# Pair phase of an RWKV-7/GLA block kernel: written-out pair loop, deferred head norm, projection work moved into the scan, turns as identity products

## The reference, cut to what matters

```python
def _rwkv_scan(r, decay, k, v, a_vec, b_vec, s0, reverse, emit):
    """RWKV-7 state recurrence S <- S diag(w) + (S a) b^T + v k^T, y = S r."""
...
decay = jnp.exp(-jnp.exp(-jax.nn.softplus(-w_log) - 0.5))
iclr = jax.nn.sigmoid(lp["a_a0"] + jnp.einsum("btdr,drc->btdc", la, lp["a_a2"]))
kk = kk * lax.rsqrt(jnp.sum(kk * kk, axis=-1, keepdims=True) + 1e-12)
...
mu = jnp.mean(wkv, axis=-1, keepdims=True)
var = jnp.mean(jnp.square(wkv - mu), axis=-1, keepdims=True)
y_a = ((wkv - mu) * lax.rsqrt(var + A_LN_EPS)).reshape(bsz, t, A_WIDTH) * lp["a_lnx_g"] + lp["a_lnx_b"]
bonus = jnp.einsum("bthn,btdhn,hn->bth", f["r"], f["k"], lp["a_r_k"])[..., None] * f["v"]
y_a = (y_a + bonus.reshape(bsz, t, A_WIDTH)) * jax.nn.silu(f["z_a"])
```

## Time and profile before

| What | us |
|---|---|
| median of three runs | 2912.06 |
| the profiled execution, own time | 2906.06 |
| its span, first to last instruction | 2904.3 |
| TensorE busy in the span | 2618.7 (90%) |
| GpSimd, ScalarE, VectorE busy | 1421.1, 1114.5, 1013.6 |
| first product of pair 0 (L551) | 314.9 |
| last VectorE operation of pair 7 (L1059) | 1104.1 |
| mean granted clock of TensorE | 0.956 of full speed |

### The profile page before, as it was taken

The page is one execution under the profiler, slowest core; times in us unless marked ns, Lnnn a source line. Parts: engine busy times, 40 slices in busy tenths (PEclk is TensorE's granted clock), DMA queues, the critical chain, the costliest instruction groups (busy, mean ns, idle before and its releaser), DMA issues.

```text
span 2904.3 us, 68141 instructions
## 1 busy us (share of the span) xinstructions
PE 2618.7 (90%) x27478; PEld 2337.1 (80%) x27478; DVE 1013.6 (35%) x1692; ACT 1114.5 (38%) x1642; POOL 1421.1 (49%) x623
## 2 busy tenths in 40 slices
PE   7997879887987978999999997998999989999998
PEld 5665766665775667877899996998998989999997
DVE  0215845555564542333211113333332133233311
ACT  0103333333333323344444434544444454454443
POOL 0006212122121103444688885776666867776785
PEclk9999989899998978999999998999999999999999
DMA  8682111111111102222555552444444534444453
GB/s 302 225 280 89 62 40 40 54 41 45 41 48 45 38 17 68 87 87 87 194 180 182 186 182 73 154 163 152 150 140 137 186 111 159 166 152 159 159 176 121
DMA packets 97980, 361.43 MB, mean 124 GB/s; under 512 B 10880, under 2 KB 12032, under 8 KB 97440
## 3 DMA queue, kind: packets, MB, share of 16 engines
q1 hardware_dynamic: 97488, 355.85, 36.7%
q10 hardware_dynamic: 336, 3.15, 0.3%
HBM read 356.85 MB, written 2.10 MB: 124 GB/s over the span
## 4 chain that ended last, share of the span: by engine, by line
PE 70%; issue 7%; ACT 6%; DVE 5%; POOL 4%; ACTq 0%; DVEq 0%; POOLq 0%
PE ps L193 16%; PE ps L195 15%; PE ps L194 15%; PE ps L488 4%; POOL wlo L181 3%; PE ps L490 3%; PE ps L489 3%; ACT whi L171 2%; PE ps L580 1%; PE ps L567 1%; PE ps L551 1%; PE ps L1483 1%; PE ps L622 1%; DVE W L881 1%; POOL alo L1517 1%
## 5 line engine op out<-in xcount | busy, mean ns | idle before, releaser
L181 POOL TENSOR_TENSOR wlo<-raw,whi 128x1024 fp32r<-128x1024 f32 x566 | 1371.7, 2442 | 1407.0 <-ACT whi L171 1397.2
L193 PE MATMUL ps<-ahi,whi 128*128 128x256 f32 (+1 forms) x3760 | 1118.8, 298 | 66.9 <-POOL wlo L181 29.9
L194 PE MATMUL ps<-alo,whi 128*128 128x256 f32 (+1 forms) x3760 | 1099.5, 292 | 0.0
L195 PE MATMUL ps<-ahi,wlo 128*128 128x256 f32 (+1 forms) x3760 | 1099.1, 292 | 0.0
L193 PEld LDWEIGHTS ps<-ahi,whi 128*128 128x128 f32 x3760 | 728.9, 194 | 102.2 <-POOL wlo L181 38.0
L171 ACT ACTIVATE whi<-raw 128x1024 fp32r<-128x1024 f32 x566 | 585.4, 1054 | 431.0 <-PE ps L195 260.1
L195 PEld LDWEIGHTS ps<-ahi,wlo 128*128 128x128 f32 x3760 | 729.8, 194 | 10.0
L194 PEld LDWEIGHTS ps<-alo,whi 128*128 128x128 f32 x3760 | 730.1, 194 | 9.6
L488 PE MATMUL ps<-ahi,whi 128*128 128x256 f32 (+1 forms) x512 | 206.7, 404 | 0.7 <-ACT W L787 0.7
L312 PE MATMUL ps<-raw,small 128*2 128x128 f32 x1536 | 174.0, 276 | 21.9 <-DMA raw<-stream 14.3
L312 PEld LDWEIGHTS ps<-raw,small 128*2 128x2 f32 x1536 | 131.0, 86 | 65.1 <-DMA raw<-stream 14.8
(11 more groups left out here) (303 smaller groups left out, 2947.2 us busy)
## 6 DMA issues: line engine op xcount, KB each, us to landing
raw<-stream SPq DMA_DIRECT2D x662, 512.0 KB, 3.3
W<-xT SPq DMA_DIRECT2D x1, 4096.0 KB, 17.9
XR<-xT ACTq DMA_DIRECT2D x1, 2048.0 KB, 7.6
outT<-XR SPq DMA_DIRECT2D x4, 512.0 KB, 2.7
W<-pair_par SPq DMA_DIRECT2D x8, 146.0 KB, 2.9
cns<-consts SPq DMA_DIRECT2D x1, 1120.0 KB, 5.3
cns<-consts ACTq DMA_DIRECT2D x1, 896.0 KB, 10.1
W<-gk_w ACTq DMA_DIRECT2D x1, 128.0 KB, 2.4
```

What stands on the lines that cost most here:

```text
L181: nc.gpsimd.tensor_tensor(wlo[slot], raw[slot], whi[slot].bitcast(F32), ALU.subtract).then_inc(lo_done, 1)
L193: nc.tensor.matmul(out, whi[slot][:, k, :], mh, start=first and k == 0, stop=False)
L194: nc.tensor.matmul(out, whi[slot][:, k, :], ml, start=False, stop=False)
L195: ins = nc.tensor.matmul(out, wlo[slot][:, k, :], mh, start=False, stop=last and k == UK - 1)
```

## The change

The loops over pairs become Python loops, so that every pair is straight code on every engine except GpSimd's. AL and RHO, the parameters and the decays get two buffers each, by the pair's parity; the other AL buffer serves as X, and TW (the decay's logarithm) shares the buffer of the next pair's AL. The ScalarE copy of the parameters goes away, SP loads them straight into the buffer in front of the pair's fifth unit. The parts:

- **Norm.** The tail's operations of pair i-1 stand in the inverse of pair i: sum and deviation between the maskings, mean behind the third square, variance in level 1, logarithm behind the first turned copies, exponential before the copy of BE, the gated result in level 3. Five VectorE operations become three.
- **Inverse.** A level multiplies MB by X first and turns X behind it; the turn is sixteen 64x64 products with an identity per direction into banks 6 and 7 (one half bank for both directions, so the second turn waits for the copy of the first). BE, KA and V are turned by the same kind of products (32, 32 and 16). No projection piece stands in the inverse, and of VectorE's next-pair work none but six of the twelve operations of the value convolution.
- **Scan.** All 48 pieces, in the portions of FILL. The low-rank products come in two halves (w before the scan, a in step 1). Decays, both other convolutions, key norm, AL, RHO and DECS stand between the state updates. The next taken-in products (L640) move behind the state update. The bonus product stands before the scan.

```diff
+        FILL = ((3, 2, 3), (3, 2, 3), (3, 2, 3), (3, 2, 3), (1, 1, 2), (1, 1, 2), (1, 1, 2), (1, 3, 0))
-            def turn(d):
-                for b in range(4):
-                    ins = nc.tensor.transpose(ps[:, 2 + 2 * d, P * b:P * b + P], X[:, d, P * b:P * b + P], ident)
-                ins.then_inc(R["t_mm"].sem, 1)
+            def turn(d):
+                for h, a, e, b in cells():
+                    o = (h * 2 + a) * C
+                    ins = nc.tensor.matmul(ps[side(e), 6 + b, o:o + C], X[side(b), d, cell(h, a, e)],
+                                           ident[side(b), side(b)], start=True, stop=True)
+                ins.then_inc(R["t_mm"].sem, 1)
+            def to_tokens(vec):
+                for d in range(2):
+                    for c in range(8):
+                        for h in range(2):
+                            o = (d * 4 + c // 2) * C
+                            ins = nc.tensor.matmul(ps[side(c % 2), h, o:o + C], vec[side(h), d, chunk(c)],
+                                                   ident[side(h), side(h)], start=True, stop=True)
             square(KA, AL, 6).then_inc(R["prod_k"].sem, 1)
-            fill(10)
+            if i:
+                nc.tensor.matmul(ps[:, 0, 0:T], headw, ysum, start=True, stop=True).then_inc(R["mean_mm"].sem, 1)
             R["ev_mb"].wait(pe, i * 2 + 2)
-            for d in range(2):
-                R["ev_x"].wait(pe, i * 2 + d + 1)
-                turn(d)
             for lv in range(1, LEVELS + 1):
                 for d in range(2):
-                    R["xt_ev"].wait(pe, i * 10 + (lv - 1) * 2 + d + 1)
+                    if lv == 1:
+                        R["ev_x"].wait(pe, i * 2 + d + 1)
+                    else:
+                        R["x_up"].wait(pe, i * 8 + (lv - 2) * 2 + d + 1)
                     apart(pe)
                     ...
+                    if lv == 1 and d == 0:
+                        R["ev_mk"].wait(pe, i * 2 + 2)
+                    elif d == 0:
+                        R["xt_ev"].wait(pe, i * 10 + (lv - 1) * 2)
+                    else:
+                        R["xt_ev"].wait(pe, i * 10 + (lv - 1) * 2 + 1)
+                    apart(pe)
+                    turn(d)
+                if lv == 1 and i:
+                    R["dsq"].wait(pe, i)
+                    nc.tensor.matmul(ps[:, 0, T:], headw, ytmp, start=True, stop=True).then_inc(R["var_mm"].sem, 1)
...
+                if q == 1 and j < PAIRS:
+                    R["tw_ok"].wait(pe, j * 2 + 2)
+                    pe_lora_out(pe, j, 1)
+                fill(FILL[q][0])
                 R["rhs_ev"].wait(pe, i * 8 + q + 1)
...
+                fill(FILL[q][1])
                 R["u_ev"].wait(pe, i * 8 + q + 1)
...
+                if q == 4 and j < PAIRS:
+                    pe_knorm(pe, j)
+                fill(FILL[q][2])
-            R["ys_ok"].wait(pe, i + 1)
-            nc.tensor.matmul(ps[:, 4, 0:T], headw, ysum, start=True, stop=True).then_inc(R["mean_mm"].sem, 1)
-            fill(2)
...
-            R["lnv"].wait(pe, i + 1)
-            with pe.Fori(0, PAIRS - 1) as i:
-                pe_pair(pe, i, proj(pe, i + 1), i + 1)
-            pe_pair(pe, PAIRS - 1, iter(()), None)
+            for i in range(PAIRS):
+                pe_inverse(pe, i)
+                pe_scan(pe, i, proj(pe, i + 1) if i + 1 < PAIRS else iter(()))
```

VectorE in the scan of pair i (j is the next pair), and ScalarE in its steps 3 to 6:

```diff
+            state(0)
+            dve_decay(dve, j)
+            state(1)
+            go(conv_k, 10)
+            state(2)
+            go(conv_k, 2)
+            dve_keys(dve, j)
+            go(conv_r, 5)
+            state(3)
+            go(conv_r, 4)
+            state(4)
+            dve_norm_k(dve, j)
+            dve_beta(dve, j)
+            dve_keyed(dve, j)
+            state(5)
+            dve_alpha(dve, j)
+            dve_rho(dve, j)
+            state(6)
+            dve_bonus_in(dve, j)
+            go(conv_v, 6)
...
+            rhs(4)
+            act_ksq(act, j)
+            solved(4)
+            act_hi(act, j + 1, 0)
+            act_norm_ln(act, j)
+            rhs(5)
+            act_norm_exp(act, j)
+            solved(5)
```

More of the change, by code:

```diff
@@ L407, in build @@
         dd = "p (d t) -> p d t"
-        AL = area(1024).rearrange(dd, d=2)
-        RHO = area(512).rearrange(dd, d=2)
+        turns = [area(1024).rearrange(dd, d=2) for _ in range(2)]
+        halves = [area(512) for _ in range(2)]
         KA = area(1024).rearrange(dd, d=2)
@@ L625, in pe_pair, with pe_scan, fill @@
                     ins.then_inc(R["x_mm" if lv < LEVELS else "xtf_mm"].sem, 1)
-                fill(1)
-                if lv < LEVELS:
-                    for d in range(2):
-                        R["x_up"].wait(pe, i * 8 + (lv - 1) * 2 + d + 1)
-                        turn(d)
-                    fill(1)
-            R["vt_ok"].wait(pe, i + 1)
-            if j is not None:
-                pe_decay(pe, j)
-            R["xtf"].wait(pe, i * 2 + 2)
+        def pe_scan(pe, i, feed):
+            j = i + 1
+            AL, RHO = turns[i % 2], halves[i % 2].rearrange(dd, d=2)
+            def fill(n):
+                for _ in range(n):
+                    next(feed, None)
             def taken_in(q):
@@ L650, in pe_pair @@
                 if q:
+                    R["taken"].wait(pe, i * 7 + q)
                     R["st_ok"].wait(pe, i * 7 + q)
@@ new lines, in pe_pairs, with image @@
+            for i in range(PAIRS):
+                pe_inverse(pe, i)
+                pe_scan(pe, i, proj(pe, i + 1) if i + 1 < PAIRS else iter(()))
+            R["ys_ok"].wait(pe, PAIRS)
+            nc.tensor.matmul(ps[:, 0, 0:T], headw, ysum, start=True, stop=True).then_inc(R["mean_mm"].sem, 1)
+            R["dsq"].wait(pe, PAIRS)
+            nc.tensor.matmul(ps[:, 0, T:], headw, ytmp, start=True, stop=True).then_inc(R["var_mm"].sem, 1)
+        def image(bank):
+            return ps[:, bank, 0:T].rearrange("p (y x) -> p y x", y=4)
@@ L838, in act_pair @@
[L838 to L850 removed]
+                nc.scalar.activation(UU.rearrange("p (h v) -> p h v", h=2), ps[:, 2:4, C:2 * C], ACT.Copy)\
+                    .then_inc(R["u_ev"].sem, 1)
@@ new lines, in act_scan @@
+            if j == PAIRS:
+                for q in range(8):
+                    rhs(q)
+                    solved(q)
+                return
+            rhs(0)
+            act_tanh_w(act, j)
+            solved(0)
+            rhs(1)
+            act_hi(act, j, 4)
+            solved(1)
+            act_tanh_a(act, j)
+            rhs(2)
+            act_pad_k(act, j)
+            solved(2)
+            act_hi(act, j, 5)
+            act_exp_neg(act, j)
+            rhs(3)
+            act_hi(act, j, 6)
@@ new lines, in act_pairs @@
+        def act_pairs(act):
+            R["pad_zero"].wait(act, 3)
+            R["kconst"].wait(act, 3)
+            act_hi(act, 0, 3)
+            act_tanh_w(act, 0)
+            act_hi(act, 0, 4)
+            act_tanh_a(act, 0)
+            act_hi(act, 0, 5)
+            act_exp_neg(act, 0)
+            act_exp(act, 0)
+            act_pad_k(act, 0)
+            act_hi(act, 0, 6)
+            act_hi(act, 0, 7)
+            act_pad_r(act, 0)
+            act_ksq(act, 0)
+            act_hi(act, 1, 0)
+            act_hi(act, 1, 1)
+            act_pad_v(act, 0)
+            act_norm_ln(act, 0)
+            act_norm_exp(act, 0)
+            act_hi(act, 1, 2)
+            for i in range(PAIRS):
+                act_inverse(act, i)
+                if i + 2 <= PAIRS:
+                    act_hi(act, i + 1, 3)
+                act_scan(act, i)
+            act_ysum(act, PAIRS - 1)
+            act_square(act, PAIRS - 1)
+            act_var_ln(act, PAIRS - 1)
+            act_var_exp(act, PAIRS - 1)
@@ new lines, in dve_scan @@
+            if j == PAIRS:
+                for q in range(7):
+                    state(q)
+                return None
+            state(0)
[13 more added lines that the diff above has]
+            state(5)
```

601 lines of the change are left out of this document (317 added, 284 removed), and 8 rows, old and new, of the table names.

## The result

The changed kernel takes 2983.55 us (median of 4 runs, 2980.50 to 2987.91), the kernel before 2910.97 beside it (4 runs, 2909.09 to 2913.11): ratio 1.025, 95% interval 1.0232 to 1.0268. It is slower by 72.6 us. The forecast was 2882.6, between 2815 and 2950: wrong in sign, and outside the range. So a difference between runs of two groups is known to 1 or 2 us only.

The account below looks back on a forecast made before the run. TensorE was taken as the bound, busy 90% of the span, with 16 us of waits in 102. Gains of 3.5 a pair (24.5), 3.0 in pair 7 and 2 in front of pair 0 made 29.5: 2882.6 us, range 2815 to 2950.

Parts of the forecast that it names:

- The tail and the jump: End of each pair: the 11.53 us tail goes, gaining 8.4 a pair, 4.5 of it the jump to the loop's head.
- What they buy is the order: Inverse levels: identity products let the turn no longer stand in front of MB times X, and use other banks.
- the identity products at 0.5 a pair: Inverse levels: products with an identity replace transposes, 1.09 for 1.04 per level; taken as 0.5 us a pair, inside the walk.
- "issue" of 2.8 in the inverse: New inverse: waits for nothing the profile shows, 2.8 us, from pair 7's straight code losing 1.6, 0.8 and 0.4.
- The clock at 2.0: New inverse: lower clock costs 2.0 us, taken from pair 7's inverse at clock 0.89.
- the slower rival: Clock falls in the inverse: inverse 49, period 109, total 2960; wins if granted clock is below 0.75; chance 0.23.
- The inverse at 37.8: New inverse per pair: walk 33.0, "issue" 2.8 and clock 2.0 make 37.8, against 29.3: a loss of 8.5.
- the walk itself (33.0): Operation-by-operation count of the new inverse without fill: 33.0 us, of it 24.4 products and 8.6 waits.
- The scan at 60.4: New scan per pair: 23.2 without pieces, 60.7 with them, taken as 60.4 us.
- The stall of 4.0 in step 5: Scan step 5: VectorE's key norm and long operations precede the state update, 6.5 against TensorE's 2.5: 4.0 us of stall.
- Whether the mean's and the deviation's work is hidden: Next inverse: the norm hides in VectorE's and ScalarE's spare time; deviation counted in the walk, rest nothing, else 2 to 4.
- The waits vanish (0.22): Rival: VectorE and ScalarE keep up in step 5, "issue" stays at 1.2; period 90.5, total 2829; chance 0.22.

Follow-up runs that it names:

- Run 1: Kernel before with the pair loop written out on SyncE, TensorE, ScalarE and VectorE, nothing else changed: 2880.86 us, ratio 0.9896.
- run 2: Changed kernel with turns and token turns as full-width transposes again, each direction in its own bank: 2900.59 us, 0.9955 of before.
- run 9: Changed kernel plus 2048 records of unread small products behind the last pair, written out (57.92 us) and again as a loop (39.31 us): 3083.65 us.
- runs 7 and 8: VectorE's sixth and seventh state updates moved earlier among its scan operations, in run 6 (2884.28 us) and in the changed kernel (2962.60 us).
- run 11: Run 6 with VectorE's new scan order and receptance taps spread, then three pieces moved ahead of level 1 and banks reassigned: 2835.60 us, 0.9736 of before.
- run 5: Run 1 with its turns of X made as 16 products with half of the identity instead of four transposes: 2912.17 us, 1.0001 of before.
- run 6: Run 2 with 16 of 48 pieces moved into the inverse's levels, two bank choices changed, key tile copied a step earlier: 2905.48 us, 0.9976 of before.
- run 4: Changed kernel with 200 more TensorE semaphore increments a pair, 25 in each step of the scan: 3085.12 us.
- run 3: Changed kernel with 200 more TensorE semaphore increments a pair, 40 in each level of the inverse: 3178.15 us.

## Why the prediction was wrong

By its own steps:

- **The tail and the jump** (8.4 a pair, 4.5 of it the jump): the jump is right. Run 1 gives 31.6 us for it, forecast 31.5. The other 3.9 have no run of their own.
- **"What they buy is the order"; the identity products at 0.5 a pair.** This is the step that failed. I priced 16 small products by TensorE's time for them (1.09 for 64 records, 1.04 for eight transposes). That part was a small miss: TensorE is busy for 12.2 us less in run 2, 1.5 a pair. The instructions were not counted: 840 more a pair, in the one stretch from which every piece had been taken. The small turns cost 83 us in all, 10.4 a pair (run 2, at most 5.0 of the 83 for the shared banks), more than the whole loss of 72.6, and run 9 shows why: small products written out get 256 instructions each 3.47 or 3.75 us and use them up in 2.10.
- **"issue" of 2.8 in the inverse**, taken from pair 7: 9.7 in the pair at 760.29 (all gaps but the first). The row was read as a cost of pair 7's straight code, a constant, when it was the supply of a bare inverse with some 840 instructions fewer. The last sentence of the forecast named this case ("over 6 a pair ... the forecast is wrong by that much"); it should have been a rival with a price. The earlier trace rows had half of the numbers: 64 records in 1.09 us are 128 instructions, and the earlier trace rows show squares that lose time with no one to wait for. The pace of the supply stood in no row.
- **The clock at 2.0**: 4.2, by the records. After the waits of 2.48 and 3.03 the products run at close to half the pace. Sets of 32 in one inverse of the kernel after, the first two at full pace, the others behind the second wait:

```profile
780.77 0.68 PE L597 MATMUL ps<-W 64*64 64x64 f32 x32
781.24 0.68 PE L562 MATMUL ps<-cns,W 64*64 64x64 f32 x32
...
797.73 1.09 PE L597 MATMUL ps<-W 64*64 64x64 f32 x32
798.58 1.09 PE L562 MATMUL ps<-cns,W 64*64 64x64 f32 x32
```

A set starts 0.47 us after the last one in the first two, 0.85 in the others; over 766.41 to 772 and 796.83 to 801, where the granted clock is 0.50 and 0.59, that makes the 4.2, an estimate. The granted clock over the inverse was 0.88, forecast 0.9; the slower rival wanted less than 0.75. So the sign of that rival came true, by another mechanism. Half pace under a low clock is what it had reckoned with (the first square of the earlier trace rows, 1.40 for 41, ran at a granted clock of 0.50), but here it holds in two stretches of 5.6 and 4.2 us, a small part of the loss.
- **The inverse at 37.8** was 45.1 in the pair at 760.29, up to the low-rank products that the forecast put to the scan; 6.9 of "issue" and 2.2 of clock are more than the difference of 7.3, so the walk itself (33.0) was about 2 too long.
- **The scan at 60.4** was 64.1 in that pair (805.42 to 869.51). The stall of 4.0 in step 5 was right (longest 4.1 at L687) and runs 7 and 8 price it at 3.0 a pair. "Nothing" for the low-rank products' wait was 1.05 us, on VectorE's half parameters (L1018), and up to 2.0 in other pairs. The other 2.6 were not taken apart by any run.
- **Whether the mean's and the deviation's work is hidden**: in part. No wait of TensorE is put down to them, and the logarithm stands inside the next inverse. But VectorE stands for 0.95 us until the mean product is done and takes 0.42 for the deviation (763.96 in the kernel after), both ahead of the masks of X, and TensorE waits 2.48 for these. The walk had counted the deviation, with 6.4 to the first product of level 1 where it took 6.1.
- **The waits vanish (0.22)** did not happen: "issue" stood at 9.7 in the inverse at 760.29 and the stall of step 5 at 4.1. It gave the identity products nothing for the clock, and the runs show no difference that could be put down to them: full pairs' inverses had clock 0.91 with transposes (run 2) and 0.88 and 0.89 with products, pair 7's the other way round, 0.86 and 0.89, and the waits differ in each.

In sum: unrolling -31.6 (run 1), bare inverse, hidden norm, step 5 and the new orders together +19.7 (run 2 less run 1), small turns +83.0: 2983.6 from 2912.5, each step measured by leaving the others as they were in that row of runs, not in every order. Without the small turns the forecast of 2882.6 would still have been 18 us too low (run 2, 2900.59), and its sign right by 12 us.

## What to carry to other kernels

Count instructions, not only engine time: where a stretch of straight code used 256 instructions of TensorE in 2.10 us, it went on only every 3.47 or 3.75 (run 9; 5.1 and 7.0 were seen while weights were loaded), and four wide operations in place of sixteen narrow ones were worth 78 to 83 us at nearly the same engine time (run 2, busy for 12.2 less). Long products spread between short ones can pay twice, as cover for waits (run 11, 27.6 us less) and as time for the supply (run 5, 5.6 us for 8.3); moving them together for their own better price gives both up. And when work is moved out from between one engine's updates, look at what then waits for that engine (run 6 lost by VectorE's order what it had won, 53.9 us of waits for 38.0).

## What the hardware did that I had not expected

- The blocks: 256 instructions, one 16 KB packet, 3.47 or 3.75 us apart, with 2.10 us of products in each (run 9). In the changed kernel, while weights are loaded too, gaps were 3.03 and 4.94 us (796.83, 687.88). TensorE took 2.10 us for a block and the supply at least 3.47, so the rest, 1.38 or 1.65, is standing time.
- The loop over 64 records (run 9) brought one packet in, at its start, for 32 rounds, and costs 0.18 us a round; the loop over the body of a pair cost 4.5 us a round (run 1).
- Semaphore increments on TensorE cost 63 ns each in rows of 25 (run 4) and 122 to 140 in rows of 40 (run 3; 5.6 us a row), several times a small product's 17; with single ones between two sets (774.25 to 775.21 in the kernel after) 32 records still start 0.49 and 0.47 us apart.
- The product with XT in the fifth level, whose output goes to one bank instead of two, takes 1.96 us for 60 records (801.72 in the kernel after, at a granted clock of 1.00) where the earlier trace rows have 1.09 for 64 records of the other kind. The kernel before has the same (L624, 2.08 for 64 at 767.22). The two operands are swapped there too, and no run here tells which of the two it is.
